# ScalarE instead of VectorE scales and shifts transposed activations as they leave PSUM

## What is computed

```python
h = rms_norm(x, norm_mix) * (1.0 + sc_a) + sh_a
(cq, ckv, kr, fq, fk, fv, ff,
 nq, nkc, nvc, nks, nvs, nkw, nvw, ng) = jnp.split(h @ w_in, split_points, axis=-1)
...
q = (rms_norm(cq, q_norm) @ w_uq).reshape(B, S, MLA_HEADS, MLA_NOPE + MLA_ROPE)
kv = (rms_norm(ckv, kv_norm) @ w_ukv).reshape(B, S, MLA_HEADS, MLA_NOPE + MLA_V)
...
o = jnp.concatenate([rms_norm(o_mla, g_mla), rms_norm(o_fox, g_fox), rms_norm(o_nsa, g_nsa)], axis=-1)
x = x + gt_a * (o @ w_out)
h = rms_norm(x, norm_mlp) * (1.0 + sc_m) + sh_m
u = jnp.square(jax.nn.relu(h @ mlp_w1))
return x + gt_m * (u @ mlp_w2)
```

## Time and profile before

| what | value |
|---|---|
| median of 3 runs | 2694.66 us (2694.21 to 2696.88) |
| the profiled execution's own time | 2697.63 us |
| span of its trace | 2695.6 us |
| mean granted TensorE clock | 0.96 of full speed |
| busy: PE, DVE, ACT | 91%, 68%, 41% of the span |
| DMA | 636.00 MB, mean 236 GB/s |

### The profile page before, as it was taken

How to read it: one execution, slowest core, us unless ns; L and a number is a source line. 1 busy time by engine, 2 the same in 40 slices (tenths; PEclk the granted TensorE clock), 3 DMA queues, 4 the chain that set the end, 5 groups by cost and what they waited for, 6 DMA issues and landing times.

```text
span 2695.6 us, 29460 instructions
## 1 busy us (share of the span) xinstructions
PE 2444.9 (91%) x11212; PEld 2005.1 (74%) x11212; DVE 1832.5 (68%) x2229; ACT 1115.7 (41%) x1490; POOL 19.2 (1%) x44
## 2 busy tenths in 40 slices
PE   2678779987999999999998988998899999999997
PEld 2567668766887888888887767876687788888886
DVE  6877777667877677677675776766767745545454
ACT  2134444433353443444443454442444344354453
POOL 1000000000000000000000000000000000000000
PEclk9788989989999999999998999998999999999999
DMA  8868886558788888888884676655668755556554
GB/s 299 310 222 262 268 275 202 177 192 272 245 289 293 296 296 301 267 291 286 282 301 136 199 259 217 203 177 188 205 219 294 244 187 187 190 186 198 186 190 145
DMA packets 318899, 636.00 MB, mean 236 GB/s; under 512 B 20460, under 2 KB 41384, under 8 KB 317864
## 3 DMA queue, kind: packets, MB, share of 16 engines
q1 hardware_dynamic: 314432, 625.49, 69.8%
q10 hardware_dynamic: 4328, 8.64, 0.9%
HBM read 631.95 MB, written 2.10 MB: 235 GB/s over the span
## 4 chain that ended last, share of the span: by engine, by line
PE 46%; issue 31%; DVE 14%; DMA 5%; ACT 3%; POOL 0%; ACTq 0%; DVEq 0%; POOLq 0%
PE acc L1462 10%; PE acc L1463 10%; PE acc L1464 10%; DVE ada_acc L980 6%; DMA ada_raw<-in_ada_w 4%; DVE w_lo L1017 3%; PE pair L1462 3%; PE pair L1463 3%; PE pair L1464 3%; PE bank_T L1383 1%; ACT w_hi L672 1%; PE bank_T L1345 1%; DMA w_raw<-in_nsa_cmp_k_w 1%; PE pair L1508 1%; PE pair L1516 1%
## 5 line engine op out<-in xcount | busy, mean ns | idle before, releaser
L1017 DVE TENSOR_TENSOR w_lo<-w_raw,w_hi 128x1024 fp32r<-128x1024 f32 (+5 forms) x832 | 970.8, 1185 | 337.3 <-ACT w_hi L672 335.4
L672 ACT ACTIVATE w_hi<-w_raw 128x1024 fp32r<-128x1024 f32 (+5 forms) x832 | 834.8, 1026 | 661.5 <-DMA w_raw<-in_mlp_w 220.5
L1462 PE MATMUL acc<-w_hi,hT_hi 128*128 128x512 f32 (+3 forms) x1536 | 621.5, 405 | 58.7 <-DVE w_lo L1017 51.7
L1463 PE MATMUL acc<-w_hi,hT_lo 128*128 128x512 f32 (+3 forms) x1536 | 599.9, 391 | 0.0
L1464 PE MATMUL acc<-w_lo,hT_hi 128*128 128x512 f32 (+3 forms) x1536 | 599.4, 390 | 0.0
L980 DVE SCALAR_TENSOR_TENSOR ada_acc<-ada_raw,silu_c,ada_acc 128x1024 f32<-128x1024 f32 x300 | 384.0, 1280 | 106.9 <-DMA ada_raw<-in_ada_w 105.3
L1462 PEld LDWEIGHTS acc<-w_hi,hT_hi 128*128 128x128 f32 x1536 | 299.7, 195 | 127.2 <-issue 45.8
L1464 PEld LDWEIGHTS acc<-w_lo,hT_hi 128*128 128x128 f32 x1536 | 298.7, 194 | 58.1
L1463 PEld LDWEIGHTS acc<-w_hi,hT_lo 128*128 128x128 f32 x1536 | 299.5, 195 | 53.0 <-issue 1.9
L1462 PE MATMUL acc<-w_hi,uT_hi 128*128 128x512 f32 (+1 forms) x728 | 289.1, 397 | 15.1 <-DVE w_lo L1017 15.0
L1464 PE MATMUL acc<-w_lo,uT_hi 128*128 128x512 f32 (+1 forms) x728 | 283.4, 389 | 0.0
(11 more groups left out here) (238 smaller groups left out, 2079.6 us busy)
## 6 DMA issues: line engine op xcount, KB each, us to landing
w_raw<-in_mlp_w SPq DMA_DIRECT2D x512, 512.0 KB, 5.3
ada_raw<-in_ada_w SPq DMA_DIRECT2D x320, 512.0 KB, 5.2
w_raw<-in_w_in SPq DMA_DIRECT2D x112, 512.0 KB, 4.8
arena<-in_ada_w SPq DMA_DIRECT2D x64, 512.0 KB, 6.2
w_raw<-in_w_out SPq DMA_DIRECT2D x64, 512.0 KB, 5.3
w_raw<-in_nsa_cmp_k_w SPq DMA_DIRECT2D x32, 512.0 KB, 5.2
w_raw<-in_nsa_cmp_v_w SPq DMA_DIRECT2D x32, 512.0 KB, 5.3
w_raw<-in_w_in SPq DMA_DIRECT2D x16, 388.0 KB, 4.5
```

The source lines that it names most:

```text
L672: a.activation(w_hi[:, Q % RING, 0:nk, 0:n], w_raw[:, Q % RING, 0:nk, 0:n], ACT.Copy).then_inc(hi_done, 1)
L1017: v.tensor_tensor(w_lo[:, Q % RING, 0:nk, 0:n], w_raw[:, Q % RING, 0:nk, 0:n], w_hi[:, Q % RING, 0:nk, 0:n].bitcast(F32), ALU.subtract).th ...
L1462: pe.matmul(o, st_hi[:, kt + k, tok], wh, start=first and k == 0, stop=False)
L1463: pe.matmul(o, st_lo[:, kt + k, tok], wh, start=False, stop=False)
```

## The change

On ACT, `split_hi` now begins with the two 128 by 256 instructions that take the transposed blocks out of PSUM: `Copy` with a scale for each partition, or `Identity` with a scale and a shift for each partition. It waits for the full bank itself, frees the bank, waits for its own write and then makes the high part as before. On DVE, `split` keeps only the subtraction. For `n1` and `n2` ACT also waits on a new semaphore `columns_done`, which DVE raises after the scale columns; in exchange DVE no longer waits for its own write there. `kcT` and `vcT` keep their old instructions. The helper `gains` is moved up so that ACT can use it.

```diff
-            def split_hi(l, name, v, dst):
+            def split_hi(l, name, v, dst, scales, shifts=None):
+
+                bank, free = T_BANK[l, name], t_free[T_BANK[l, name]]
+                act.wait_ge(*t_is_full(l, name))
+                for k in range(2):
+                    if shifts is None:
+                        ins = a.activation(v[:, k, :], BANKS[bank][:, k, :], ACT.Copy, scale=scales[:, k:k + 1])
+                    else:
+                        ins = a.activation(v[:, k, :], BANKS[bank][:, k, :], ACT.Identity, scale=scales[:, k:k + 1],
+                                           bias=shifts[:, k:k + 1])
+                ins.then_inc(free, 1)
                 act.wait_ge(*t_is_free(l, name))
                 a.activation(dst, v, ACT.Copy).then_inc(v_hi, 1)
...
                 elif name[:3] in ("n1_", "n2_"):
                     k = int(name[3:])
-                    split_hi(l, name, y_half(l, f"{name[:2]}y{k // 2}", k % 2), hT_hi[:, 2 * k:2 * k + 2, :])
+                    mul, cols = (scale_A, ada_A) if name[1] == "1" else (scale_M, ada_M)
+                    act.wait_ge(columns_done, COLUMNS_NO[l, name[1], k // 2])
+                    split_hi(l, name, y_half(l, f"{name[:2]}y{k // 2}", k % 2), hT_hi[:, 2 * k:2 * k + 2, :],
+                             mul[:, 2 * k:2 * k + 2], cols[:, 0, 2 * k:2 * k + 2])
...
-                link(v.scalar_tensor_tensor(mul[:, 4 * b:4 * b + 4], cols[:, 1, 4 * b:4 * b + 4], 1.0,
-                                            gains(la, at + 4 * b, 4), ALU.add, ALU.mult))
+                v.scalar_tensor_tensor(mul[:, 4 * b:4 * b + 4], cols[:, 1, 4 * b:4 * b + 4], 1.0,
+                                       gains(la, at + 4 * b, 4), ALU.add, ALU.mult).then_inc(columns_done, 1)
...
-            def split(l, name, dst_v, scales, shifts, dst_lo, hi_src):
-                bank = BANKS[T_BANK[l, name]]
-                dve.wait_ge(*t_is_full(l, name))
-                for k in range(2):
-                    if shifts is None:
-                        ins = v.tensor_scalar(dst_v[:, k, :], bank[:, k, :], scales[:, k:k + 1], None, ALU.mult)
-                    else:
-                        ins = v.tensor_scalar(dst_v[:, k, :], bank[:, k, :], scales[:, k:k + 1], shifts[:, k:k + 1],
-                                              ALU.mult, ALU.add)
-                ins.then_inc(t_free[T_BANK[l, name]], 1)
+            def split(l, name, v_, dst_lo, hi_src):
+
                 dve.wait_ge(v_hi, split_value(l, name))
-                v.tensor_tensor(dst_lo, dst_v, hi_src.bitcast(F32), ALU.subtract).then_inc(split_done, 1)
+                v.tensor_tensor(dst_lo, v_, hi_src.bitcast(F32), ALU.subtract).then_inc(split_done, 1)
```

More of the change, by code:

```diff
@@ L315, in ada_of @@
     return BLOCK_NO[l, "G" if name[:3] == "gta" else "H", int(name[3]) // 2]
+COLUMNS_NO = {}
+for la, kind, b in ADA_BLOCKS:
+    if kind in "AM":
+        COLUMNS_NO[la, "1" if kind == "A" else "2", b] = len(COLUMNS_NO) + 1
 ADA_LAST = {}
@@ L481, in trunk @@
         dve_own, pool_own = sem("dve_own"), sem("pool_own")
+        columns_done = sem("columns_done")
         silu_e, ang_ready, trig_done = sem("silu_e"), sem("ang_ready"), sem("trig_done")
@@ L521, in sums_no, with gains @@
             return 10 * l + 2 * ("cq", "ckv", "omla", "onsa", "ofox").index(name) + 2
+        def gains(l, at, n):
+            return gcols[:, l * GAINS + at:l * GAINS + at + n]
         def unit(l, u):
@@ L724, in t_out @@
                     j = int(name[-1])
-                    split_hi(l, name, y_half(l, "cq", j), uT_hi[:, 2 * j:2 * j + 2, :])
+                    split_hi(l, name, y_half(l, "cq", j), uT_hi[:, 2 * j:2 * j + 2, :], gains(l, G_Q + 2 * j, 2))
                 elif name == "ckv0":
-                    split_hi(l, name, y_half(l, "ckv", 0), uT_hi[:, 4:6, :])
+                    split_hi(l, name, y_half(l, "ckv", 0), uT_hi[:, 4:6, :], gains(l, G_KV, 2))
                 elif name in ("kcT", "vcT"):
@@ L729, in t_out @@
                     j = ("kcT", "vcT").index(name)
-                    split_hi(l, name, blk, BLK[j][:, 0:2048].rearrange("p (l r) -> p l r", l=32)[:, :, 0:32])
+                    act.wait_ge(*t_is_free(l, name))
+                    a.activation(BLK[j][:, 0:2048].rearrange("p (l r) -> p l r", l=32)[:, :, 0:32], blk,
+                                 ACT.Copy).then_inc(v_hi, 1)
                 elif name in ("ofox0", "ofox1"):
                     j = int(name[-1])
-                    split_hi(l, name, FQ[:, 2 * j:2 * j + 2, :], hT_hi[:, 4 + 2 * j:6 + 2 * j, :])
+                    split_hi(l, name, FQ[:, 2 * j:2 * j + 2, :], hT_hi[:, 4 + 2 * j:6 + 2 * j, :],
+                             gains(l, G_OUT + 4 + 2 * j, 2))
@@ L734, in t_out @@
                 elif name in ("omla0", "omla1"):
                     j = int(name[-1])
-                    split_hi(l, name, MQ[:, 2 * j:2 * j + 2, :], hT_hi[:, 2 * j:2 * j + 2, :])
+                    split_hi(l, name, MQ[:, 2 * j:2 * j + 2, :], hT_hi[:, 2 * j:2 * j + 2, :],
+                             gains(l, G_OUT + 2 * j, 2))
                 elif name.startswith("onsa"):
                     j = int(name[-1])
-                    split_hi(l, name, ONSA_T[:, 2 * j:2 * j + 2, :], hT_hi[:, 8 + 2 * j:10 + 2 * j, :])
+                    split_hi(l, name, ONSA_T[:, 2 * j:2 * j + 2, :], hT_hi[:, 8 + 2 * j:10 + 2 * j, :],
+                             gains(l, G_OUT + 8 + 2 * j, 2))
@@ L914, in bc @@
                 return ap.broadcast_to(shape)
-            def gains(l, at, n):
-                return gcols[:, l * GAINS + at:l * GAINS + at + n]
             dve.wait_ge(t_full[0], 1)
@@ L1152, in t_out @@
                     j = int(name[-1])
-                    split(l, name, y_half(l, "cq", j), gains(l, G_Q + 2 * j, 2), None,
-                          uT_lo[:, 2 * j:2 * j + 2, :], uT_hi[:, 2 * j:2 * j + 2, :])
+                    split(l, name, y_half(l, "cq", j), uT_lo[:, 2 * j:2 * j + 2, :], uT_hi[:, 2 * j:2 * j + 2, :])
                 elif name == "ckv0":
-                    split(l, name, y_half(l, "ckv", 0), gains(l, G_KV, 2), None, uT_lo[:, 4:6, :], uT_hi[:, 4:6, :])
+                    split(l, name, y_half(l, "ckv", 0), uT_lo[:, 4:6, :], uT_hi[:, 4:6, :])
                 elif name in ("kcT", "vcT"):
@@ L1178, in t_out @@
                     src = {"ofox": FQ, "omla": MQ, "onsa": ONSA_T}[name[:4]][:, 2 * j:2 * j + 2, :]
-                    split(l, name, src, gains(l, G_OUT + k0, 2), None, hT_lo[:, k0:k0 + 2, :], hT_hi[:, k0:k0 + 2, :])
+                    split(l, name, src, hT_lo[:, k0:k0 + 2, :], hT_hi[:, k0:k0 + 2, :])
                 elif name[:3] in ("n1_", "n2_"):
                     k = int(name[3:])
-                    mul, cols = (scale_A, ada_A) if name[1] == "1" else (scale_M, ada_M)
-                    split(l, name, y_half(l, f"{name[:2]}y{k // 2}", k % 2), mul[:, 2 * k:2 * k + 2],
-                          cols[:, 0, 2 * k:2 * k + 2], hT_lo[:, 2 * k:2 * k + 2, :], hT_hi[:, 2 * k:2 * k + 2, :])
+                    split(l, name, y_half(l, f"{name[:2]}y{k // 2}", k % 2), hT_lo[:, 2 * k:2 * k + 2, :],
+                          hT_hi[:, 2 * k:2 * k + 2, :])
                 elif name[:3] in ("ada", "nex"):
```

## The result

After the change the kernel takes 2677.69 us (median of 4 runs, 2675.58 to 2678.57), where the kernel before took 2695.77 us (median of 4 runs, 2694.21 to 2701.87; three of them are those of the table above). The medians are 18.1 us apart. The ratio is 0.9928 with a 95% interval of 0.9910 to 0.9945, so 19.4 us were won, or 14.8 to 24.3. A second comparison with more runs of the kernel before (experiment 9) gives 0.9945 (0.9927 to 0.9964), 14.8 us (9.7 to 19.7). The forecast of 2684.0 us lies 6.3 us too high, its range of 2674 to 2691 holds the result, and "faster" is what happened. The profiled execution took 2677.5 us (span 2675.4), against 2697.6 (span 2695.6) before.

The account below looks back on a forecast made before the run. PE was busy 91% of the span, so only its 9% standing still, where it waits for a split, could move. The terms 2.6 + 3.1 + 1.0 + 4.0 = 10.7 us gave 2694.7 - 10.7 = 2684.0 us, range 2674 to 2691.

Parts of the forecast that it names:

- The main reason: All 54 splits: ACT is there first, DVE second, so an instruction moved to ACT never starts later; no loss expected.
- Term 1: First stage, 50 to 157 us: ACT's second split overlaps DVE's first subtraction, 0.65 us a block, 2.6 us for four.
- Term 2: Around cq and ckv: PE's waits go, 2.0 us in the first layer and 1.1 us in layer 1, together 3.1 us.
- Term 3: At omla1: high part done 0.5 us earlier, passing through to PE's 3.31 us wait; two layers, 1.0 us.
- Term 4: At onsa3, ofox0, ofox1: late DVE saves up to 4.7 us a layer; 2.0 taken because of DMA, 4.0 us in all.
- The named signs of the opposite case: Longer DVE waits for ada_raw between 575 and 620 us, or a PE pause of equal length a few pieces later.
- Term 5: Other first norm splits, 1.72 against 1.69 us, and remaining splits ending under PE's running matmuls: nothing.
- One named sign: At every second norm split: DVE's wait for ACT shorter than 0.70 us; at cq1, ckv0, ofox0, ofox1: gone.
- All of it comes: Whole kernel: per-partition operands cost nothing and the DMA engines follow; 20.4 us won, 2674 us; chance 0.25.
- Freed time turns into waits: Late outputs, omla1, layer 1's cq and ckv win nothing, DVE waiting longer for DMAs; 4.6 us, 2690 us; chance 0.20.
- ACT out of PSUM is slow: All splits: slow ACT lengthens latency, deciding from 2.5 us; 2700 us needs 2.9 us; chance 0.03.

Follow-up runs that it names:

- experiment 9: The full change once more, unaltered, timed in five rounds beside the others and the kernel before: 2677.27 us, ratio 0.9945.
- starred traces: Profiled executions of kernels in which the splits of the stretch in question are moved to ACT; no single time.
- Experiment 6: The changed kernel with a third ACT pass of 256 columns in each split, into a tile nothing reads: 2686.48 us, 0.9973 against the kernel before.
- the outputs alone: Against the kernel before, only the splits of omla, onsa and ofox moved to ACT, in both layers: 2684.88 us, ratio 0.9971.
- Experiment 5: The changed kernel with two spare DVE multiplications in each split before its wait for the high part: 2680.21 us, 0.9951 against the kernel before.
- experiment 11: Against the kernel before, only the splits of onsa3, ofox0 and ofox1 moved to ACT, in both layers: 2685.06 us, ratio 0.9978.
- experiments 7 and 8: The kernel before and the changed kernel, both unaltered, one more profiled execution each: 2696.46 and 2676.23 us.
- Experiment 4: Against the kernel before, only the splits of n2 in both layers and n1 in layer 1 moved to ACT: 2691.58 us, ratio 0.9997.

## Why the prediction was right, and where a size was off

**The main reason held.** In the kernel before, ACT is first at every split and DVE second. No part that was moved alone measured slower than before. The time itself decides little: the first comparison lies nearer to the rival that expects all of it (2674) than to the forecast (2684), the second nearer to the forecast (14.8 us against 10.7 and 20.4). The terms have to be judged one by one.

**Term 1, first stage, 2.6 us.** The mechanism and size are shown: 0.71 us a block in the rows, and over 46 to 183 us a median of -2.9 us in the six starred traces without extra work, against -0.9 in the five others, 2.0 us. Experiment 6 shows the factor of two on the latency. Up to 157 us, where the fourth block ends, the medians differ by 3.0 us (-3.7 against -0.7), so 1 us is gone again by 183. The timed runs of this part alone (0.5 us) can't tell it from nothing, and don't exclude it.

**Term 2, `cq` and `ckv`, 2.0 and 1.1 us.** 2.2 and 1.6 us in every trace with these splits moved (1.7 and 1.4 where DVE keeps its work) and 0.0 in every other; 3.2 us timed. In layer 0 it stays (2.2 us up to 240 us too). In layer 1 the traces don't show that it stays: from 1495 to 1590 us the median is -1.5 with these splits moved and -2.1 without, and both groups spread over 3 us or more. So the 1.6 us are won where they were forecast, and whether they reach the end is open.

**Term 3, `omla1`, 0.5 us a layer.** PE's wait is 2.80 to 2.82 us in the four traces of the changed kernel and of the outputs alone, and 3.31 to 3.33 in the seven with `omla1` not moved, in both layers alike: 0.5 us each, as forecast. The stretches around it win more by the medians (1.6 us from 490 to 563, 1.8 us from 1768 to 1844). The 1.1 and 1.3 us beyond this wait are in no term, and where they come from is open.

**Term 4, the late outputs, 2.0 us a layer: this is the term that was mis-sized.** It took 2.0 between the ends 0 and 4.7, because a DVE that is earlier would ask for tiles that the DMA engines couldn't bring much sooner. By 563 to 671 us six traces with these splits moved have a median of -4.4 us and five without have -0.1: 4.3 us. In layer 1 it is -4.05 against -0.7: 3.4. Together 7.7 us instead of 4.0. That rests on the traces: timed alone it is 5.9 us, with an interval (2.4 to 9.2) that holds both. The named signs of the opposite case did not appear: DVE waits hardly longer for `ada_raw`, and PE's pauses a piece later (0.47 and 0.83 us) are less than half of the 1.45 and 1.76 us that went. Who waited for whom at the late outputs in the kernel before, 575 to 620 us:

```profile
DVE ada_acc L980 <- DMA ada_raw<-in_ada_w: 7.5, 6, 2.7
...
PE acc L1462 <- DVE w_lo L1017: 3.0, 2, 1.8
...
PE pair L1462 <- DVE w_lo L1017: 1.8, 2, 1.5
```

and in the changed one, 566 to 610 us:

```profile
DVE ada_acc L1004 <- DMA ada_raw<-in_ada_w: 7.9, 7, 2.4
...
PE acc L1476 <- DVE w_lo L1041: 2.1, 2, 1.3
...
PE pair L1476 <- DVE w_lo L1041: 0.5, 1, 0.5
```

DVE waits 0.4 us longer for DMAs, and PE 2.2 us shorter for DVE. A busy share of 0.91 to 0.93 of the DMA engines did not mean here that they set the pace. The better sign was the DMA queue's own waits. In the kernel before, over 563 to 671 us, SP waits for DVE before it may load the next tile:

```profile
SPq L577 <- DVE ada_acc L980: 57.8, 23, 13.5
```

and in the changed kernel, over 554 to 658 us:

```profile
SPq L586 <- DVE ada_acc L1004: 54.3, 23, 13.8
```

23 tiles in both, each asked for when DVE has used one up. DVE waits for these tiles too (7.5 us above), so the loading and DVE's work form one loop through a ring of two buffers; the time taken off DVE shortened the loop instead of running into a limit. This view was read for the first stage before and not for this one; that was the omission. Experiment 5 agrees, and sets DVE's freed time apart from the earlier scaling: with two multiplications of 0.50 us per split put back on DVE, and ACT's part still moved, this stretch wins 1.0 us instead of 4.4, and the one in layer 1 2.4 instead of 4.05.

**Term 5, the other norms, nothing.** 0.8 us with an interval on both sides of zero.

**One named sign was wrong.** The prediction looked for a wait of DVE shorter than 0.70 us at every second split of a norm. Its own numbers say otherwise: the second subtraction was to start 3.33 - 1.72 = 1.61 us after the first, which takes 0.69, so a wait of about 0.9 us was to be expected, and it is 0.88 in the first stage. Nor is the wait gone at `cq1` (0.19 us in layer 0, 0.70 in layer 1); at `ckv0`, `ofox0` and `ofox1` it is. The terms don't use this sign.

**The sum.** With the measured numbers in its place (the stretches', and PE's wait for term 3): 2.0 + 2.2 + 1.6 + 2 x 0.5 + 4.3 + 3.4 = 14.5 us, against 10.7 forecast and 14.8 timed in experiment 9. The difference of 3.8 us to the forecast is term 4 (3.7), with the small ones cancelling. That 14.5 comes so near to 14.8 is partly luck: without the 1.6 us of layer 1 that may not last it is 12.9, with the 1.1 and 1.3 us around `omla1` it is 16.9, and the timed interval is 9.7 to 19.7. The first comparison's 19.4 us is more than any of these; its interval begins at 14.8. For the rest the traces show no place, unless it is the stretch from 207 to 490 us, which moves by itself.

**The rivals.** "All of it comes" (20.4 us) had term 4 right, 2 x 4.7, and the prices wrong: the first operand per partition costs 471 - 377 = 94 ns and the second 84 ns. "Freed time turns into waits" (4.6 us) is excluded by both comparisons of the full change and by experiment 11, whose interval begins at 2.4 us where this rival gives nothing. "ACT out of PSUM is slow" is excluded by 471 and 555 ns; experiment 6 made ACT's pass half as long again, and the kernel was still faster than before.

## What to carry to other kernels

When two engines hand a block to and fro, look for which one is idle at the start of each handover: giving it the first step too cost no latency here though it is no faster (1.71 us against 1.69), and the gain came from the second block, which it starts while the other engine still has the first. A step taken off an engine that arrives last was won nearly in full (4.3 and 3.4 of 4.7 us), and a high busy share of the DMA engines was no reason to discount it where their queue waited for that engine. Compare parts of a few us over the stretch in which they lie, in several traces with the part and without it: the whole run's time moves more by itself.

## What the runs showed that was not expected

An unchanged kernel does not repeat itself from stretch to stretch. The same piece of work ran in the kernel before as

```profile
240.00:264.00 24.00, 21.59 (x88) 17.77 (x89) 16.14 (x23) 10.00 (x12) 0.00 (x0) 0.86 0.78 255
```

and in the changed one as

```profile
236.00:256.60 20.60, 18.31 (x87) 15.15 (x88) 16.10 (x23) 10.23 (x12) 0.00 (x0) 1.00 0.86 296
```

The granted clock is 0.86 in the one and 1.00 in the other (1.00 is the upper of its two levels, 2.4 GHz; 0.86 mixes both), and the DMA engines moved 255 and 296 GB/s. The 3.4 us between them look like a gain, but the clock is not the kernel's own (experiments 7 and 8). Experiment 4, in which none of the nearby splits is moved, wins 8.2 us over 207 to 490, and experiment 9, in which all are, loses 2.6. The two traces of the kernel before differ by 3.4 us over 207 to 490, and the second one gives 5.5 us back between 1583 and 1740. The changed kernel's six timed runs in experiment 9 lie in two groups, 2672.5 to 2674.3 and 2680.2 to 2685.4 us. Why a run falls in the one or the other is not known.
